# Low parts of sixteen weight pieces of a two-block transformer kernel: ScalarE's negated rounding and an adding DMA in place of plain fp32 products and VectorE's subtraction

## The reference

```python
h = modulate(rmsnorm(x, norm_mix_g), sh_m, sc_m)
proj = h @ w_in                                  # 256 x 1024 times 1024 x 5192
q, k, v, qi, ki, wi, u, ga, gb = split(proj)
score = einsum(wi, relu(qi . ki / 8)) with a causal mask; sel = top 64 of each row
y_attn = softmax(q . k_sel / 8 - slope * dist) @ v_sel @ w_attn_proj    # 8 heads of 64
y_conv = silu(layernorm(depthwise_conv31(a * sigmoid(g)))) @ w_conv_proj
merged = sigmoid(ga) * y_attn + sigmoid(gb) * y_conv
```

## Time and profile before

| | |
|---|---|
| median of three runs | 949.65 us (948.02 to 950.03) |
| the profiled execution: its own time, and its span | 949.03 us, 947.2 us |
| TensorE (PE) busy | 908.8 us, 96% |
| VectorE (DVE) busy | 627.1 us, 66% |
| ScalarE (ACT) busy | 457.7 us, 48% |
| POOL busy | 31.7 us, 3% |
| DMA traffic | 178.10 MB, mean 188 GB/s |

### The profile page before, as it was taken

How to read it: one execution, slowest core, us unless ns; L and a number is a source line. 1 busy time by engine, 2 the same in 40 slices (tenths; PEclk the granted TensorE clock), 3 DMA queues, 4 the chain that set the end, 5 groups by cost and what they waited for, 6 DMA issues and landing times.

```text
span 947.2 us, 11986 instructions
## 1 busy us (share of the span) xinstructions
PE 908.8 (96%) x4235; PEld 730.6 (77%) x4235; DVE 627.1 (66%) x1022; ACT 457.7 (48%) x711; POOL 31.7 (3%) x42
## 2 busy tenths in 40 slices
PE   3999999899999999999999999999999999999997
PEld 3877754678788888887888777788888788888785
DVE  3897999988755555676757545788645665555444
ACT  0554523365554444543754555574535565555432
POOL 2110000010000000000000000000000000000000
PEclk9999999999999999999999999999999999999999
DMA  9999324566485555475555343455552376554531
GB/s 333 349 387 345 125 89 149 200 235 202 151 265 182 177 178 185 181 268 208 171 185 180 131 148 119 134 188 190 178 178 59 122 228 190 189 188 178 178 134 44
DMA packets 103030, 178.10 MB, mean 188 GB/s; under 512 B 6318, under 2 KB 52635, under 8 KB 102986
## 3 DMA queue, kind: packets, MB, share of 16 engines
q1 hardware_dynamic: 96138, 151.23, 47.7%
q0 software_dynamic: 6848, 26.28, 7.4%
HBM read 176.39 MB, written 1.05 MB: 187 GB/s over the span
## 4 chain that ended last, share of the span: by engine, by line
PE 72%; DVE 13%; issue 8%; DMA 4%; ACT 2%; SPq 0%; POOL 0%; DVEq 0%; POOLq 0%; ACTq 0%
PE bank L569 18%; PE bank L571 17%; PE bank L570 17%; PE bank L983 10%; DVE conv_out L1930 5%; DVE w_lo L1712 2%; ACT w_hi L1243 1%; DVE ada_acc L1788 1%; DMA raw_weights<-in_w_in 1%; DMA tap_rows<-in_w_dw 1%; PE bank L962 1%; PE bank L648 1%; DMA ada_raw<-in_w_ada 1%; PE bank L640 1%; PE bank L1186 1%
## 5 line engine op out<-in xcount | busy, mean ns | idle before, releaser
L1712 DVE TENSOR_TENSOR w_lo<-raw_weights,w_hi 128x1024 fp32r<-128x1024 f32 x267 | 324.2, 1222 | 225.7 <-ACT w_hi L1243 224.5
L1243 ACT ACTIVATE w_hi<-raw_weights 128x1024 fp32r<-128x1024 f32 x267 | 280.5, 1057 | 283.0 <-PE bank L571 200.5
L569 PE MATMUL bank<-w_hi,a_hi 128*128 128x512 f32 x808 | 323.4, 400 | 3.2 <-issue 1.3
L571 PE MATMUL bank<-w_hi,a_lo 128*128 128x512 f32 x808 | 315.9, 391 | 0.0
L570 PE MATMUL bank<-w_lo,a_hi 128*128 128x512 f32 x808 | 315.4, 390 | 0.0
L569 PEld LDWEIGHTS bank<-w_hi,a_hi 128*128 128x128 f32 x808 | 152.2, 188 | 38.8 <-issue 6.5
L571 PEld LDWEIGHTS bank<-w_hi,a_lo 128*128 128x128 f32 x808 | 152.0, 188 | 32.7
L570 PEld LDWEIGHTS bank<-w_lo,a_hi 128*128 128x128 f32 x808 | 152.4, 189 | 29.7 <-issue 0.2
L983 PE MATMUL bank<-w_hi,ff_hi 128*128 128x512 f32 x176 | 55.1, 394 | 0.8 <-DVE hidden_rows L2210 0.5
L983 PE MATMUL bank<-w_lo,ff_hi 128*128 128x512 f32 x176 | 54.3, 390 | 0.0
L983 PE MATMUL bank<-w_hi,ff_lo 128*128 128x512 f32 x176 | 54.2, 389 | 0.0
(11 more groups left out here) (264 smaller groups left out, 846.0 us busy)
## 6 DMA issues: line engine op xcount, KB each, us to landing
raw_weights<-in_w_in SPq DMA_DIRECT2D x40, 1024.0 KB, 5.0
raw_weights<-in_w_ffn_in SPq DMA_DIRECT2D x44, 512.0 KB, 4.5
raw_weights<-in_w_gate_up SPq DMA_DIRECT2D x44, 512.0 KB, 4.5
ada_start<-in_w_ada POOLq DMA_DIRECT2D x11, 1024.0 KB, 11.1
raw_weights<-in_w_ffn_out SPq DMA_DIRECT2D x9, 1024.0 KB, 4.8
raw_weights<-in_w_down SPq DMA_DIRECT2D x9, 1024.0 KB, 4.8
ada_raw<-in_w_ada POOLq DMA_DIRECT2D x8, 1024.0 KB, 8.3
raw_weights<-in_w_out SPq DMA_DIRECT2D x8, 1024.0 KB, 5.0
```

The lines of the kernel that those rows point to most:

```text
L569: pe.matmul(ps, hi[:, kt, ts], wh, start=start, stop=False)
L571: return pe.matmul(ps, lo[:, kt, ts], wh, start=False, stop=stop)
L1243: act.activation(w_hi[:, slot, 0:m], raw[:, b % RAW, half * PIECE:half * PIECE + m], ACT.Copy)\
L1712: dve.tensor_tensor(w_lo[:, slot, 0:m], raw[:, b % RAW, half * PIECE:half * PIECE + m], w_hi[:, slot, 0:m], ALU.subtract).then_inc(lo_read ...
```

## The change

No piece is multiplied in plain fp32 any more. All sixteen gate pieces, 25 to 40, are split in a new way. ScalarE writes the negated rounded weights to the slot of `w_lo` (`Copy` with scale -1), then the rounded ones to `w_hi`; POOL then issues a DMA that reads the same 512 KB of `w_in` from memory once more and adds it to what stands in `w_lo` (`accum_op` add), which leaves the low part. VectorE has no `conv` for these pieces; before, it had one for 35 to 40. TensorE waits for the adding DMA and for `w_hi`, and uses `mm3`. A raw block is free for the next load when ScalarE has read it, not when TensorE has used it. POOL issues `w_ada` blocks 16 and 17 after the adding DMAs of pieces 34 and 36.

```diff
-NATIVE_FIRST, NATIVE_LAST = 25, 34
+ADDED = tuple(range(25, 41))
...
@@ SP: load
-                if native(q):
-                    sp.wait_ge(piece_used, q + 1)
-                else:
-                    sp.wait_ge(lo_ready, split_count(q) + 1 + i * step)
+                if added(q):
+                    sp.wait_ge(hi_ready, q + 1)
+                if not added(q) or not added(q - 1):
+                    sp.wait_ge(lo_ready, residue_count(q) + (not added(q)) + i * step)
@@ POOL
-            if n == 17:
-                pool.wait_ge(piece_used, NATIVE_LAST + 1)
...
-        for n in range(14, 20):
+        for n in range(14, 16):
+            ada_block(n)
+        for p in ADDED:
+            s, j = (p - P_IN1) // 4, (p - P_IN1) % 4
+            pool.wait_ge(sem["negated"], added_count(p) + 1)
+            pool.dma_start(w_lo[:, p % RING, :].rearrange("p (k n) -> p k n", k=2),
+                           w2["w_in"].rearrange("(k p) n -> p k n", p=P)[:, 2 * j:2 * j + 2, IN1_COLS[s]:IN1_COLS[s] + W],
+                           accum_op=ALU.add).then_inc(added_landed[p % RING], 16)
+            if p in (34, 36):
+                ada_block(p // 2 - 1)
+        for n in range(18, 20):
             ada_block(n)
@@ TensorE: piece
-            if native(p):
-                b, half = block_of(p)
-                pe.wait_ge(raw_landed[b % RAW], 16 * (b // RAW + 1))
+            if added(p):
+                pe.wait_ge(hi_ready, p + 1)
+                pe.wait_ge(added_landed[p % RING], 16 * (1 + sum(q < p and q % RING == p % RING for q in ADDED)))
             else:
-                pe.wait_ge(lo_ready, split_count(p) + 1 + i * 8)
+                pe.wait_ge(lo_ready, residue_count(p) + 1 + i * 8)
...
-                    if native(p):
-                        w = raw[:, b % RAW, half * PIECE + kk * W:half * PIECE + (kk + 1) * W]
-                        last = pe.matmul(ps, f_h1[:, kt, t * P:(t + 1) * P], w, start=(kt == 0), stop=(kt == 2 * n - 1))
-                    else:
-                        last = mm3(ps, kbase + kt, t, hi, lo, wh[:, kk, :], wl[:, kk, :], kt == 0, kt == 2 * n - 1)
+                    last = mm3(ps, kbase + kt, t, hi, lo, wh[:, kk, :], wl[:, kk, :], kt == 0, kt == 2 * n - 1)
@@ ScalarE: conv
-                if native(q):
-                    continue
...
                 if q >= RING:
-                    act.wait_ge(piece_used, slot_freed(q) + i * 8)
+                    act.wait_ge(piece_used, q - RING + 1 + i * 8)
+                if added(q):
+                    act.activation(w_lo[:, slot, :], raw[:, b % RAW, half * PIECE:(half + 1) * PIECE], ACT.Copy, scale=-1.0)\
+                        .then_inc(sem["negated"], 1)
                 m = KD * SMALL if q == P_SMALL else PIECE
                 act.activation(w_hi[:, slot, 0:m], raw[:, b % RAW, half * PIECE:half * PIECE + m], ACT.Copy)\
                     .then_inc(hi_ready, 1)
@@ VectorE: conv
-                if native(q):
+                if added(q):
                     continue
...
-                dve.wait_ge(hi_ready, split_count(q) + 1 + i * 8)
+                dve.wait_ge(hi_ready, q + 1 + i * 8)
```

More of the change, by code:

```diff
@@ L111, in last_piece_of, with added, added_count, residue_count @@
     return 2 * b + (b < 2)
-def native(p):
-    return NATIVE_FIRST <= p <= NATIVE_LAST
-def split_count(p):
-    return p - min(max(p - NATIVE_FIRST, 0), NATIVE_LAST + 1 - NATIVE_FIRST)
-def slot_freed(p):
-    return max(q for q in range(p) if not native(q) and split_count(q) == split_count(p) - RING) + 1
+def added(p):
+    return p in ADDED
+def added_count(p):
+    return sum(q < p for q in ADDED)
+def residue_count(p):
+    return p - added_count(p)
 N_H1, N_H2, N_FINAL1, N_M2, N_CR, N_F2, N_FINAL2 = range(7)
@@ L268, in build @@
     second_landed = [S(f"second_half_landed{i}") for i in range(RAW)]
+    added_landed = [S(f"added{i}_landed") for i in range(RING)]
     hi_ready, lo_ready, piece_used = S("hi_ready"), S("lo_ready"), S("piece_used")
@@ L588, in piece @@
                 pe.wait_ge(hidden[0], hidden[1] + i * 4)
-            slot = split_count(p) % RING
+            slot = p % RING
             wh = w_hi[:, slot, :].rearrange("p (k n) -> p k n", k=2)
@@ L927, in project @@
                     if t == 0:
-                        pe.wait_ge(lo_ready, split_count(q) + 1)
+                        pe.wait_ge(lo_ready, residue_count(q) + 1)
                         pe.wait_ge(*after(tag, "lo", j + 1))
-                    slot = split_count(q) % RING
+                    slot = q % RING
                     wh = w_hi[:, slot, :].rearrange("p (k n) -> p k n", k=2)
@@ L977, in output @@
             def output(kt, t, then=None, count=1):
-                slot = split_count(p + kt) % RING
+                slot = (p + kt) % RING
                 wh, wl = w_hi[:, slot, :], w_lo[:, slot, :]
@@ L991, in feed_forward @@
             for kt in range(2):
-                pe.wait_ge(lo_ready, split_count(p + kt) + 1)
+                pe.wait_ge(lo_ready, residue_count(p + kt) + 1)
                 output(kt, 1)
```

6 lines of the change are left out of this document (3 added, 3 removed).

## The result

The changed kernel takes 956.88 us (median of 4 runs, 955.3 to 958.64) against 948.89 us for the kernel before, measured beside it (948.02 to 950.03): a ratio of 1.0076, 95% interval 1.006 to 1.0091. It is 0.8% slower, where 945.1 us was forecast, and 956.88 lies just above the range given (944 to 956). The profiled execution has a span of 953.6 us against 947.2, and its own time is 955.5 us.

A forecast was written before the change was run, and what follows sets the result against it. VectorE was taken to bound up to step 12, TensorE after it. -5.65 (VectorE) + 0.95 (order of step 11) + 0.2 (TensorE's step 11) = -4.5 us gave 945.1 us against the median 949.65; range 944 to 956.

The forecast's parts named there:

- VectorE: Six `w_lo` passes removed, five ahead of the maximum of step 12, which moves from 184.10 to 178.45: -5.65 us.
- ScalarE: 26 added passes of 0.95 us each, mostly covered within VectorE's steps of 4.1 us.
- the order of step 11: In step 11 a second ScalarE pass stands ahead of the `pT` that TensorE's step 12 waits for: +0.95 us.
- TensorE and the start: TensorE keeps pace; idle more than 4 us before step 2, slow clock made good by step 11; step 11 adds 0.2 us.
- The adding DMAs: Sixteen transfers of 512 KB, 2.7 us of engine time each, landing in 6 to 8.7 us, hidden.
- rival C: Adding DMAs don't keep up, TensorE waits at pieces 29 to 40: slower, 953 at 4.8 us each, 956 at 5.1; chance 0.27.
- a room of 7.5 to 10.1: Time in us from a piece's negation to its matmuls, for its adding DMA: 10.1, least at piece 29 with 7.5.
- I count nothing for it: `w_ada` blocks and plain loads can hold up an adding DMA or two in the gate pieces' stage; taken as no cost.
- C's sub-case at twice plain: DMA load of 73.3 us binds in a stretch that is to be 66.5 long: 951.9 us; chance half of C's.
- Rivals B: Part of the gain: adding DMAs land in 9.5 to 11 us, or a long slow clock; 947 to 949.5; chance 0.12.
- D: No change: ScalarE takes VectorE's place as the bound, or its order eats the gain; 948.5 to 951; chance 0.08.
- Each us beyond 9.6 costs about three: Under B, twelve pieces from 29 on use a ring of four slots, three rounds, so late landings cost about threefold.

The follow-up runs named there:

- run without DMAs: The changed kernel without its sixteen adding DMAs, so `w_lo` keeps the negated rounded weights and TensorE waits for ScalarE's passes alone: 945.11 us, ratio 0.9943.
- the early six: The kernel before, with pieces 25 to 30 made by adding DMAs, 31 to 34 plain fp32, 35 to 40 split by VectorE: 950.6 us, ratio 1.0007.

## Why the prediction was wrong

**VectorE: right.** Steps of 4.1 us from step 7 on and a maximum of step 12 ready at 178.4, as forecast (178.5).

**ScalarE: right.** The negating pass is shown with 1.05 us and starts 0.95 ahead of the next. In the run without DMAs step 12 comes at 180.85 instead of the 181.8 worked out, so 0.95 for the order of step 11 was enough.

**TensorE and the start: right.** The gap before step 2 is 4.2 us. In the run without DMAs it is 4.8, the clock after it is 0.50 from 142 to 146 us, and step 12 is on time all the same, so the slow clock is made good.

**The adding DMAs: the step that failed.** Its size of the work was near: 2.7 us of engine time were 2.84, and from 118 to 205 us both queues together were busy for 89.5 us instead of 43.3, 46.2 more, where the sum had 43.5. (That 1.03 x 71 = 73.1 us from 118 to 189 meets the forecast's 73.3 says little: engines that never pause show a share near 1 however much is waiting.) Issue is 1.18 us, not 0.75; of the landings of 11.3 and more that is a small part. What failed is the conclusion "With 6 to 8.7 us the DMAs are hidden", and the argument that set it above rival C: "loads have a lead of one or two blocks and that queues share, so the loads would be late and not the adding DMAs". The landings of 6 to 8.7 us were worked out for one addition beside one load, although the same prediction, under C, had the engines' work at more than the time there was. With engines that hardly pause, both sorts are late: the additions with a median of 11.3 us and up to 17.4 against a room of 7.5 to 10.1, the loads with 10 to 21 us instead of 5 to 7, and the lead doesn't help, since it is spent at the start (the first load moves from 134 to 123 us) and isn't renewed. So the term "I count nothing for it" is the one that was mis-sized: it was taken as 0 and measured 11.8 us by the medians (956.9 against 945.1 without the DMAs).

**Rival C: the right mechanism, too small a chance and too low a price.** It asked for TensorE's waits at pieces 29 to 40, and they came, at 30, 35 and 37, and one more at 131.4 us, before step 0. The Trainium skill, "Collectives: The Full Stack", section "The bandwidth ceiling: the fold count and why AG ≠ RS ≠ AR", puts the adding step of a ring of cores at half the rate of a copy. The traces of this one core come near it: 2.84 us against 1.8 for the plain DMA in the same places and 1.36 by the rows of before, a factor of 1.6 to 2.1. C's sub-case at twice plain named what happened, but its 951.9 was 5 us too low.

Where the time went can be read from the changed kernel's trace beside that of the run without DMAs. Step 9 begins at 171.33 instead of 169.31, 2.0 us later, step 12 at 190.78 instead of 180.85, 9.9 later, step 15 10.3 later, and the spans differ by 10.1. So the loss is complete by step 12, and most of it falls between steps 9 and 12. There TensorE waited 2.3 + 3.4 = 5.7 us for the additions of pieces 35 and 37, and a granted clock of 0.82 over 19.45 us is worth another 3.5, while the run without DMAs has 1.00. That makes 9.2 us, an estimate, for the 7.9 that were lost there. C, which only made the traffic fit, had 6.8 us for step 12, and it came 190.78 - 181.8 = 9.0 after the forecast; the cost of the clock is what C lacked. Why one addition takes 17.4 us and not 11, when all of them share the same queues, no run shows.

That the late part is the crowded one fits the kernel before: between 155 and 205 us it already used 32.5 of 50 us, and the early six, in the emptier part, cost nothing.

**Rivals B and D** would give a part or nothing of the gain; neither happened. "Each us beyond 9.6 costs about three" isn't borne out where it was tested: the six early additions landed with a median of 9.4 us and up to 11.2, and cost nothing that can be told.

## What to carry to other kernels

When a change moves work to the DMA engines, add up their busy time in the stretch in which it falls and in the one behind it, and if the sum comes near the stretch, price every transfer there as late, the old ones too: a latency taken from a half idle queue doesn't hold. Use the new path only as far as the idle time of the engines reaches: here three of the sixteen pieces gave 3.6 us, and six gave all of it back and more. An operation that relieves one engine on paper is to be tried in its smallest useful number first.

## What the runs showed of the hardware

- An adding DMA from HBM into SBUF took 2.84 us of the 16 engines for 512 KB, 1.6 to 2.1 times a plain one (1.8 in the same places, 1.36 before), and 2.65 with the source in SBUF; all are worked out from the queues' rows. Its issue on POOL takes 1.18 us for 512 KB, 0.84 for 256 KB or with an SBUF source, and a plain one 0.70.
- In crowded queues a plain 1 MB load from SP landed 21 us after its issue instead of 7.4, and a block of `w_ada` from POOL in 10.3 instead of 5.5 (medians): both queues were late.
- After waits of 2.3 and 3.4 us TensorE's granted clock fell to 0.50, the 1.2 GHz level, and from 171.33 to 190.78 us it was 0.82.
- GpSimd's subtraction of 128 x 1024 in float32 took 2.47 us and held up a two-input tap of VectorE for about 2 us of it (2.62 us instead of 0.47). The Trainium skill, "SBUF — State Buffer", section "Who interferes with whom", says that a VectorE instruction with two SBUF inputs contends with a GpSimd instruction that reads SBUF; the trace agrees, with steps of 6.2 us instead of 4.1.
